# RWKV stage in a nine-stage layer stack: chunk problems of 64x64 in quadrants, projection tiles placed between them

## What is computed

```python
p = h @ w_in                                  # 1024 -> 3*512 (conv) + 3*512 + 32 + 32 + 96 (rwkv)
y_conv = gate_b * _short_conv(gate_c * h_in, conv_w)          # 3 taps
p_rwkv = p_rwkv + (_shift(p_rwkv) - p_rwkv) * mu_shift
log_w = -softplus(-(w0 + tanh(dw) @ w_up)) - 0.5;  decay = exp(-exp(log_w))
a = sigmoid(a0 + da @ a_up);  g = sigmoid(dg) @ g_up
kk = heads(k * k_k); kk = kk * rsqrt(max(sum(kk * kk), 1e-24))
k_h = heads(k) * (1 + (a_h - 1) * k_a)
# per token: S = S * w_t + (S @ -kk) b_t^T + v_t k_t^T ;  y_t = S r_t     (8 heads of 64)
y = groupnorm(y) * ln_w + ln_b + sum(r_h * k_h * r_k) * v_h
return concatenate([y_conv, y * g]) @ w_out
```

## Time and profile before

| | us |
|---|---|
| median of 3 runs (1709.22 to 1712.72) | 1712.7 |
| the profiled execution | 1712.08 |
| its span, first to last instruction | 1710.2 |
| TensorE matmul busy in the span | 1594.9 |
| DVE, ACT, POOL busy in the span | 822.7, 781.4, 554.6 |
| mean granted TensorE clock | 0.967 |

### The profile page before, as it was taken

The page is one execution under the profiler, slowest core; times in us unless marked ns, Lnnn a source line. Parts: engine busy times, 40 slices in busy tenths (PEclk is TensorE's granted clock), DMA queues, the critical chain, the costliest instruction groups (busy, mean ns, idle before and its releaser), DMA issues.

```text
span 1710.2 us, 27533 instructions
## 1 busy us (share of the span) xinstructions
PE 1594.9 (93%) x10808; PEld 1460.8 (85%) x10808; DVE 822.7 (48%) x1073; ACT 781.4 (46%) x1065; POOL 554.6 (32%) x224
## 2 busy tenths in 40 slices
PE   7999888698889999999998999999999999699997
PEld 7999788587779998899987789998999977589996
DVE  4444454643354443544454454444544379754443
ACT  5444436332154444544456554445544367454443
POOL 2444203123014443544424234442444400024442
PEclk9999999788899999999999999999999999899999
DMA  7545444100025444455453245553554543235542
GB/s 271 185 184 184 148 148 158 76 1 1 2 102 216 183 185 160 164 193 184 184 184 112 74 148 190 187 185 141 208 196 181 188 163 123 84 120 210 185 183 87
DMA packets 48080, 259.92 MB, mean 152 GB/s; under 512 B 5376, under 2 KB 5632, under 8 KB 27296
## 3 DMA queue, kind: packets, MB, share of 16 engines
q1 hardware_dynamic: 47664, 258.77, 41.3%
q10 hardware_dynamic: 288, 0.34, 0.1%
q0 software_dynamic: 80, 0.14, 0.0%
HBM read 258.18 MB, written 1.05 MB: 152 GB/s over the span
## 4 chain that ended last, share of the span: by engine, by line
PE 81%; DVE 8%; ACT 6%; DMA 2%; issue 1%; POOL 1%; SPq 0%; DVEq 0%; ACTq 0%; POOLq 0%
PE banks L356 72%; ACT gu_hi L327 2%; DMA raw_gu<-units_gu 1%; DVE gu_lo L336 1%; PE banks L1228 1%; DVE arena L2242 1%; PE banks L1234 1%; POOL dn_lo L349 1%; ACT arena L393 1%; DVE x L484 1%; PE banks L1201 1%; PE banks L1169 0%; PE banks L1925 0%; ACT h_hi L376 0%; PE banks L1924 0%
## 5 line engine op out<-in xcount | busy, mean ns | idle before, releaser
L349 POOL TENSOR_TENSOR dn_lo<-raw_dn,dn_hi 128x1024 fp32r<-128x1024 f32 x144 | 492.5, 3420 | 983.4 <-ACT dn_hi L332 964.6
L356 PE MATMUL banks<-h_hi,gu_hi 128*128 128x256 f32 x2256 | 642.9, 285 | 15.7 <-DVE h_lo L416 9.1
L356 PE MATMUL banks<-h_lo,gu_hi 128*128 128x256 f32 x2256 | 640.5, 284 | 0.0
L356 PE MATMUL banks<-h_hi,gu_lo 128*128 128x256 f32 x2256 | 640.4, 284 | 0.0
L336 DVE TENSOR_TENSOR gu_lo<-raw_gu,gu_hi 128x2048 fp32r<-128x2048 f32 x161 | 371.6, 2309 | 233.1 <-ACT gu_hi L327 232.8
L356 PEld LDWEIGHTS banks<-h_hi,gu_hi 128*128 128x128 f32 x2256 | 433.7, 192 | 24.1 <-issue 8.6
L356 PEld LDWEIGHTS banks<-h_lo,gu_hi 128*128 128x128 f32 x2256 | 434.0, 192 | 4.8 <-issue 0.2
L356 PEld LDWEIGHTS banks<-h_hi,gu_lo 128*128 128x128 f32 x2256 | 433.7, 192 | 0.0
L327 ACT CAST gu_hi<-raw_gu 128x2048 fp32r<-128x2048 f32 x161 | 306.1, 1904 | 59.8 <-PE banks L356 31.7
L499 ACT ACTIVATE silu<-silu 128x256 f32<-128x256 f32 x132 | 55.1, 417 | 509.2 <-DVE silu L507 509.2
L356 PE MATMUL banks<-dn_hi,act_hi 128*128 128x512 f32 x528 | 207.4, 393 | 1.7 <-POOL dn_lo L349 1.7
(11 more groups left out here) (340 smaller groups left out, 1500.3 us busy)
## 6 DMA issues: line engine op xcount, KB each, us to landing
raw_gu<-units_gu SPq DMA_DIRECT2D x161, 1024.0 KB, 6.0
raw_dn<-units_dn SPq DMA_DIRECT2D x162, 512.0 KB, 3.3
x<-x_in SPq DMA_DIRECT2D x2, 512.0 KB, 4.8
raw_gu<-units_gu SPq DMA_DIRECT2D x2, 512.0 KB, 7.2
out<-x SPq DMA_DIRECT2D x1, 1024.0 KB, 3.9
cst<-constants SPq DMA_DIRECT2D x1, 784.0 KB, 12.4
lora<-low_rank SPq DMA_DIRECT2D x1, 512.0 KB, 13.1
arena<-final_gain SPq DMA_DIRECT2D x1, 512.0 KB, 4.1
```

Source lines behind the costliest of these rows:

```text
L349: nc.gpsimd.tensor_tensor(dn_lo[:, p, 0:n], raw_dn[:, p, 0:n], dn_hi[:, p, 0:n].bitcast(F32), ALU.subtract).then_inc(dn_lo_ready, 1)
L356: ins = nc.tensor.matmul(out, a, b, start=first and i == 0, stop=last and i == 2)
```

## The change

The stage "even" is rewritten; the other eight stages are the same code.

- **Order of channels.** The units hold k first, then the low ranks (decay and rate in one tile of 96 columns, gate in another), then r, v, and the convolution's three parts. There are still 26 tiles and 8 output rows in 12 units, but a tile or a row may now be in any of the three places of a unit.
- **Front.** The input is normalized and turned by a matmul with the diagonal matrix of inverse roots (`rstd_diag`), in place of two scalings on DVE and 16 transposes.
- **Token mix.** ACT scales by 1 - mu on its way out of PSUM, DVE adds mu times the shifted tile straight from PSUM, tile by tile.
- **Decay.** `decay_in` is made in token order with its bias as one more row of weights; sums over the chunk are a product with triangular constants ("cumsum"), relative to the chunk's middle. ACT takes the exponentials from PSUM. The scan is gone.
- **Chunk algebra.** All 32 problems go in one round. Each is a 64x64 product in one quadrant of the array, the two chunks of a pair in the two row halves. Turning the inverse is a product with a 64x64 identity. The masks of the levels are applied by DVE to `x` on its way out of PSUM; POOL has only memsets left, and all `lo_dn` are DVE's.
- **Projection tiles between.** Tiles 0 to 10 come before the first level; tile 11 + l is split over level l in parts of 2, 3 and 3 of its 8 input blocks; tiles 16 to 25 stand between the steps behind the levels; all 8 output rows come last.
- **Smaller.** Token-order turns are one per level; DVE's self-waits are written only where needed; table loads of ACT are placed by hand; mean and variance, state products and y are in other banks; the convolution goes channel block by channel block.

```diff
-                  ("before", P), ("not_after", P), ("pairs", P), *((f"join{n}", P) for n in LEVELS),
+                  ("not_after", P), ("before", P), *((n, CHUNK) for n in ("before2", "not_after2", "pairs2", "eye2")),
+                  *((f"join{n}", CHUNK) for n in LEVELS),
...
-                for l, n in enumerate(LEVELS):
-                    if l:
-                        after(pool, "pe", ("x", jj, l - 1, 1))
-                    done(nc.gpsimd.tensor_tensor(flat(AO).rearrange("p (q t) -> p q t", t=P),
-                                                 flat(AB).rearrange("p (q t) -> p q t", t=P),
-                                                 eye_view(f"join{n}", 8), ALU.mult), ("ao", jj, l))
+            pool.wait_ge(squares_ready, 2 * s + 2)
+            done(nc.gpsimd.memset(u_conv[:, :, 0:2], 0.0), "pads")
+            after(pool, "pe", ("inc", NL - 1, 1))
+            done(nc.gpsimd.memset(flat(PHI), 0.0), "phi0")
+            done(nc.gpsimd.memset(arena[:, ST, 256:768], 0.0), "bd0")
...
+            after(act, "pe", "cumsum")
+            sums = banks[:, 2:6, :].rearrange("p j (m i t) -> p i j m t", m=2, i=2)
+            for name, slot, i, sign in (("e0", E0, 1, -1.0), ("em", EM, 0, 1.0), ("e1", E1, 0, -1.0)):
+                done(nc.scalar.activation(c4(slot).rearrange("p j (m t) -> p j m t", m=2), sums[:, i], ACT.Exp,
+                                          scale=sign * LOG_W), name)
+            firsts = sums[:, 1].rearrange("p j m (c t) -> p j m c t", t=CHUNK)[:, :, :, :, 0]
+            done(nc.scalar.activation(mid.rearrange("p j (m c) -> p j m c", m=2), firsts, ACT.Exp, scale=LOG_W), "mid")
+            after(act, "dve", "b")
+            for j in range(4):
+                ins = nc.scalar.activation(c4(AI)[:, j, :], c4(AI)[:, j, :], ACT.Identity, scale=pcol("k_a", j),
+                                           bias=omka[:, j:j + 1])
+            done(ins, "factor")
+            hi_gu(act, *unit(s, 3))
...
+            for l in range(NL):
+                if l < 3:
+                    copy_tok(TOKS[l])
+                if l < NL - 1:
+                    copy_m(l, 0)
+                    copy_m(l, 1)
+                evac(11 + l)
+                if l == 0:
+                    hi_dn(act, *unit(s, 4))
+                if l == 2:
+                    hi_gu(act, *unit(s, 5))
+                if l == 3:
+                    hi_dn(act, *unit(s, 5))
...
+            def level(l):
+                eights = lambda ap: ap.rearrange("p (q t) -> p q t", t=CHUNK)
+                join = const(f"join{LEVELS[l]}").rearrange("p (q t) -> p q t", q=1).to_broadcast([P, 8, CHUNK])
+                own("kt")
+                for h in range(2):
+                    after(dve, "pe", ("x", l, h))
+                    done(tt(eights(arena[:, XB, h * 512:(h + 1) * 512]), eights(banks[:, 2 + h, :]), join, ALU.mult),
+                         ("x", l, h))
+                for h in range(2):
+                    half = arena[:, MT, h * 512:(h + 1) * 512]
+                    after(dve, "pe", ("inc", l, h))
+                    own(("mt", l - 1, h) if l else "mt1")
+                    done(tt(half, half, banks[:, 4 + h, :], ALU.add), ("mt", l, h))
...
+            after(pe, "dve", "diag")
+            for b in range(4):
+                for i in range(2):
+                    for t in range(2):
+                        ins = mm(banks[:, b, i * T + t * P:i * T + (t + 1) * P], x[:, t, (2 * b + i) * P:(2 * b + i + 1) * P],
+                                 rstd_diag[:, t, :], start=True, stop=True)
+                ins.then_inc(xT_ready, 1)
...
+            def tile(i, ks=range(KD)):
+                u, place = divmod(i, 3)
+                w = (dn_weights if place == 2 else gu_weights)(pe, s, u)
+                if ks[0] == 0 and i >= 6:
+                    after(pe, *(("dve", ("mix", i - 2)) if i - 2 < MIXED else ("act", ("evac", i - 2))))
+                m = 96 if i in LOW_TILES else P
+                for k in ks:
+                    if i == 0 and k % 2 == 0:
+                        pe.wait_ge(h_lo_ready, 4 * s + k // 2 + 1)
+                    ins = three_products(tile_place(i), w((DN if place == 1 else 0) + k * m, m), (h_hi[:, k, :], h_lo[:, k, :]),
+                                         k == 0, k == KD - 1)
+                if ks[-1] == KD - 1:
+                    if place == 0:
+                        done(ins, ("tile", i))
+                    else:
+                        ins.then_inc((gu_used, dn_used)[place - 1], 1)
...
+            def scores(name, left, right, b):
+                for j, m, g, c in QUADS:
+                    t = chunk_of(2 * m + c)
+                    ins = mm(banks[rows64(c), b + g, (2 * j + m) * CHUNK:(2 * j + m + 1) * CHUNK], c4(left)[rows64(g), j, t],
+                             c4(right)[rows64(g), j, t], start=True, stop=True)
+                done(ins, name)
...
+            def by_problem(name, h, bank, left, right):
+                for q in range(8):
+                    for c in range(2):
+                        ins = mm(banks[rows64(c), bank + h, q * CHUNK:(q + 1) * CHUNK], prob(left)[rows64(c), 8 * h + q, :],
+                                 prob(right)[rows64(c), 8 * h + q, :], start=True, stop=True)
+                done(ins, name)
+            def turn_m(l, h):
+                for q in range(8):
+                    for c in range(2):
+                        ins = mm(banks[rows64(c), 6 + h, q * CHUNK:(q + 1) * CHUNK], prob(MT)[rows64(c), 8 * h + q, :],
+                                 const("eye2")[rows64(c), :], start=True, stop=True)
+                done(ins, ("m", l, h))
...
+            after(pe, "act", "iclr")
+            running = cst[:, CONST_COLS["not_after"].start:CONST_COLS["before"].stop]
+            for j in range(4):
+                for m in range(2):
+                    ins = mm(banks[:, 2 + j, m * 2 * P:(m + 1) * 2 * P], flat(SWT)[:, m * RW + j * P:m * RW + (j + 1) * P], running,
+                             start=True, stop=True)
+            done(ins, "cumsum")
...
+            after(pe, "dve", "ab")
+            tok_source = {"a": AT_, "b": BT_, "k": KT_}
+            for l in range(NL):
+                for h in range(2):
+                    after(pe, "act", ("m", l - 1, h))
+                    by_problem(("x", l, h), h, 2, AB, MI)
+                if l == 2:
+                    after(pe, "dve", "kt")
+                if l < 3:
+                    turn(TOKS[l], c4(tok_source[TOKS[l]]))
+                elif l == 3:
+                    scores("ak", KT_, AT_, 6)
...
+                    after(pe, "dve", "rt")
+                    scores("rk", KT_, RT_, 6)
+                tile(11 + l, range(0, 2))
+                for h in range(2):
+                    after(pe, "dve", ("x", l, h))
+                    by_problem(("inc", l, h), h, 4, XB, MT)
+                tile(11 + l, range(2, 5))
+                if l < NL - 1:
+                    after(pe, *(("act", ("tok", TOKS[l])) if l < 3 else ("dve", "ak")))
+                    for h in range(2):
+                        after(pe, "dve", ("mt", l, h))
+                        turn_m(l, h)
+                tile(11 + l, range(5, KD))
+            a_tok, b_tok, k_tok, v_tok = (None, *(tok(n) for n in (B_TOK, K_TOK, V_TOK)))
+            after(pe, "act", ("tok", "b"))
+            scores("rb", BT_, RT_, 2)
```

More of the change, by code:

```diff
@@ new lines, in even_act @@
+            after(act, "pe", "gate_in")
+            done(cp(split2(flat(GATE)), two(6)), "gate")
+            evac(8)
+            hi_dn(act, *unit(s, 3))
+            evac(9)
+            copy_m(-1, 0)
+            copy_m(-1, 1)
+            hi_gu(act, *unit(s, 4))
+            evac(10)
+            for l in range(NL):
+                if l < 3:
[10 more added lines that the diff above has]
+                    hi_dn(act, *unit(s, 5))
@@ new lines, in even_dve @@
+            after(dve, "pe", "rb")
+            masked(RB, 2, "not_after2", "rb")
+            lo_gu(dve, *unit(s, 6))
+            after(dve, "pe", "bonus")
+            own(("mix", 13))
+            done(tt(split2(flat(BV)), two(6), split2(flat(VC)), ALU.mult), "bv")
+            own("bv")
+            for j in range(4):
+                ins = ts(c4(BV)[:, j, :], c4(BV)[:, j, :], pcol("ln_b", j), None, ALU.add)
+            done(ins, "bv_b")
+            lo_dn(dve, *unit(s, 6))
+            after(dve, "pe", "uw")
@@ L1082, in block_diagonal @@
                 done(ins, ("bd", n))
[L1084 to L1100 removed]
+            four = lambda b, at: banks[:, b, at:at + 256].rearrange("p (j t) -> p j t", j=4)
@@ new lines, in next_state @@
+            def next_state(n):
+                own("s1" if n == 1 else ("s", n - 1))
+                done(tt(state_sum, state, four(*D_AT[n]), ALU.add), ("sd", n))
+                after(dve, "pe", ("phi_s", n))
+                own(("sd", n))
+                done(tt(state_sum, state_sum, four(5, (n - 1) * 256), ALU.add), ("sum", n))
+                own(("sum", n))
```

(50 more changed lines are left out.)

993 lines of the change are left out of this document (460 added, 533 removed).

## The result

The changed kernel takes 1619.27 us, the median of 4 runs (1617.33 to 1623.56), against 1712.71 (4 runs, 1709.22 to 1714.75): ratio 0.946, 95% interval 0.9435 to 0.9485. The forecast was 1631.0 with a range of 1606 to 1668. The profiled execution has a span of 1616.3 us, 93.9 less than before, and a mean granted clock of 0.984 against 0.967.

The account below looks back on a forecast made before the run. TensorE was taken to bound the rewritten stage: 185.1 work, 6.0 idle, 6.0 front and 7.0 slow clock made 204.1 us instead of 286, so 1631 us for the kernel, range 1606 to 1668.

Parts of the forecast that it names:

- 6.0 idle: TensorE waits in the stage: tile 9 2.5 us, fourth step 0.7, third state product 1.5, output row 0 1.3.
- 6.0 front: Start of the stage before tile 0, unchanged, and part of tile 0 at half clock: 6.0 us more in all.
- 7.0 clock: Two falls of TensorE's clock in the stage, 6.8 us long, each costing half: 7 us.
- rival of 1665: Quadrant products whose row halves write the same PSUM bank don't overlap, each runs alone: 1665 us; chance 0.12.
- TensorE's work, 185.1 forecast: Full-clock work in the stage: projections 77.0, output rows 22.4, quadrants 50.3, shape changes 7.8, other 27.6 us.
- Quadrants 50.3: Chunk algebra: 688 products at 0.055 us, 112 of d and y0 at 0.08, uw at 0.11: 50.3 us.
- Changes of array shape 7.8: Loops alternating full-width and quadrant work: some 46 changes at 0.17 us, 7.8 us in all.
- Other work 27.6: TensorE's scaled-identity products, head sums, decay, rate and gate inputs, cumulative sum, token turns, state products: 27.6 us.
- rival of 1651: DVE's or ACT's queue order sets the pace: 3 us more per step, 5 in the state chain; chance 0.08.
- rivals of 1675 and 1773: Clock falls in the quadrant stretches (1675, chance 0.13), or stays at 1.2 GHz from tile 8 on (1773, 0.03).
- what covers a step: In a doubling step the tile's three parts cover masks, adds and copies; without them up to 2 us more.
- Signs that I gave: Profile checks; wrong if step period exceeds 12 us, halves of clock appear inside steps, or TensorE idles over 15 us.

Follow-up runs that it names:

- e_warm_all: Against the changed kernel: the reordering aimed at four TensorE waits, plus 20 unused identity products ahead of the norm's wait; 1605.47 us, ratio 0.9378 to the kernel before.
- e_after_again: The changed kernel itself, unchanged, run again on the same chip as the last three experiments; 1618.72 us, ratio 0.9455 to the kernel before.

## Why the prediction was right, point by point

**Right: what bounds the stage.** TensorE's work was to be the sum and everything else cover. Its clean size is read from e_warm_all: 176.9 us busy from 205 to 384 us at clock 1.00, of which about 2 are the identity products, so 174.9. The rest of the 193.4 us of the kernel after, 18.5, is idle time and slow clock; my terms for those (6.0 idle, 6.0 front, 7.0 clock) come to 19.0. That this sum fits is luck: measured, the three are 9.4 (all the waits above but the first), 6.3 and 2.8. The parts of the gain were not taken apart by runs: undoing the overlap costs 17 us and moving the tiles out of the gaps in the steps 2 to 4, while the single round, the missing scan and the moved masks were not put back one by one.

**Right: the halves overlap** (rival of 1665). By the Trainium skill, "TensorEngine Tiling (Array Packing)", Gotcha 1: PSUM Pressure, different row tiles can't access the same bank at the same time; here they wrote the same bank on different partitions, 32 products in 2.01 us against 3.33 one at a time. The measurement decides: as a price for a shared bank it did not hold here, while whether two of them touch the bank at the same instant isn't to be seen in a trace. The price of that rival was too high as well: undoing the overlap in 15 of the 17 groups costs 17 us, not 31 to 35.

**Wrong in size: TensorE's work, 185.1 forecast, 174.9 measured.** This is 10 us of the miss of 12. Quadrants 50.3 became 46.5: the alternating pair cost 0.063, above my 0.055, but scores, phi and q, with four quadrants, 0.034 to 0.039, y0 0.034, d 0.052 where I had 0.08 for both; uw cost 3.64 as priced. The rows of before had both prices in them: 0.039 with four quadrants and two products in a row in each, 0.08 with two quadrants and four in a row. I put the difference down to order alone. How many quadrants take part counts for more, and a long run in one of them costs besides: with two in a row instead of four, the same two quadrants cost 0.052 in the new d. Changes of array shape 7.8 became about 3: a tile in three parts takes 3.25 us, whole between quadrant groups 3.06, with wide work around it 2.88, and a token turn 1.02 for 0.92; that is 0.05 to 0.1 a change, where I had taken 0.17 from one idle row. Tiles 77.0 became 75 (2.88 each). Other work 27.6 became about 29, output rows 22.4 about 22.

**Partly right: the idle places.** All four were named. Third state 1.5 and row 0 1.3 as laid out; tile 9 waited 3.4 for 2.5; the fourth step 2.5 for 0.7; and 0.7 in tile 19, with nothing that the profile shows to wait for, was not in my list. The failed step is the last: I had the ak mask late but not unit 5's split, whose ScalarE half stands behind tile 13's evacuation and whose VectorE half stands ahead of the step's first mask. Queue order set no pace elsewhere (rival of 1651): without those waits the steps run through.

**Wrong in size: the clock.** One fall of 7 us inside the stage instead of two, costing 2.8 for my 7.0; the front lost 6.3 for my 6.0, half of that slow clock, which I had put at tile 0 alone. In no quadrant stretch that followed full work did the clock fall, not even in three bare steps, so the rivals of 1675 and 1773 are out. But the clock can fall without a long wait ahead of it, as I read from the earlier trace rows: it does so in tile 7 in six of thirteen traces, behind products on few rows.

**Wrong: what covers a step.** I said that the tile's parts cover masks, adds and copies, and that a step without them costs up to 2 us more. A bare step costs its 6.9 us of TensorE and no more. The forecast didn't suffer, because with tiles a step was TensorE's work either way (10.3 for 10.2).

**A row misread.** The four instructions of 5.85 us are the bonus products (L1007), not the scaled keys; TensorE waited for them, and the rewrite moves them, so no term hangs on the name.

**Signs that I gave.** Step every 10 to 10.5: 10.3. Group of 32: 2.01 for 1.8. Mean clock over 0.95: 0.96. VectorE about 115: 112.1. POOL memsets only: yes. Gap ahead of tile 9, 2 to 3: 3.4. Stage end 409: 398.4, by the sizes above. No half clock inside the steps: so in the profile of after, but e_after_again, the same kernel, has a short one in the fourth step, behind its wait; by my own sign that speaks against me, though it costs 1.4 us only, 0.7 of it in place of a wait. TensorE idle 12.8 us in the stage, under 15.

## What to carry to other kernels

Small products in array quadrants are priced by how many quadrants take turns: order the loop so that as many as possible alternate before any repeats. Once TensorE is the bound, look for each place where it waits 1 to 4 us for weights whose splitting stands behind something slower in another engine's queue; each costs its wait and sometimes slow clock behind it (the wait ahead of tile 9 1.7 to 2.8 us more in the two profiles of the changed kernel, that of 1.5 us 1.5 more in four of eleven), and moving one weight split into idle time takes both away. When an experiment removes work and gives back less than that work, look for the late input that it used to hide.

## What the runs showed of the hardware

The price of a 64x64x64 f32 product: 0.104 us in one quadrant, 0.063 with two in turn, 0.034 with four. Two quadrants of one row half, two products in a row in each: 0.052. A change between 64x64 and 128x128 shape costs 0.05 to 0.1 us. TensorE idle for 5.6 us was followed by half clock until 4 to 6 us into the next work, and 4.6 us of throwaway products in that gap kept it at 1.00. A 1.5 us gap at the same place was followed by half clock in four of eleven traces. Behind six products on 64 and 32 rows, with no idle time of TensorE ahead of them in the stage's projections, half clock came in six of thirteen. Two VectorE subtractions from SBUF that began beside POOL's were longer by about the time shared, 0.8 and 0.5 us; VectorE work that read PSUM was not.
